# Expert weights with one run per partition, a moving operand read at a step of four, and another order of the state-space products

## The reference

```
h    = rmsnorm(x) ; proj = h @ w_in                      # 1024 x 5120
ya   = causal pooling mixer ; yb = gated MLP mixer
yc   = s5_mixer(...)                                     # 32 groups of 16 channels, 64 complex states
x    = x + (sum_k sigmoid(gate_k) * (y_k @ w_branch_k)) @ w_out
h2   = rmsnorm(x)
# 32 experts in 4 groups: best group, then 2 best experts in it, for each token
x    = x + sum over a token's 2 experts of weight * ((silu(h2 @ w_gate[e]) * (h2 @ w_up[e])) @ w_down[e])
out  = rmsnorm(x)
```

## Time and profile before

| | us |
|---|---|
| median of 3 runs | 930.88 |
| lowest and highest run | 930.44, 931.03 |
| the profiled execution | 932.56 |
| its span in the trace | 930.9 |
| PE busy in the span | 835.0 (90%) |
| DVE, ACT, POOL busy | 323.2, 195.7, 142.1 |
| bytes moved by DMA | 261.22 MB |

### The profile page before, as it was taken

The page is one execution under the profiler, slowest core; times in us unless marked ns, Lnnn a source line. Parts: engine busy times, 40 slices in busy tenths (PEclk is TensorE's granted clock), DMA queues, the critical chain, the costliest instruction groups (busy, mean ns, idle before and its releaser), DMA issues.

```text
span 930.9 us, 15236 instructions
## 1 busy us (share of the span) xinstructions
PE 835.0 (90%) x5300; PEld 569.9 (61%) x5301; DVE 323.2 (35%) x604; ACT 195.7 (21%) x289; POOL 142.1 (15%) x239
## 2 busy tenths in 40 slices
PE   7999999999999999989889998899999887777850
PEld 6888888868876888885555554555555444343420
DVE  4899996731524246265101111110101101010106
ACT  5633353222432233141000000000000000000002
POOL 4341601000000000012122221122112121212100
PEclk9999999999999999999999999999999999999995
DMA  8693224523224945049999999999999999999926
GB/s 263 148 186 111 75 66 44 167 69 113 91 90 153 401 148 225 1 160 387 402 417 420 418 418 420 421 420 419 418 420 419 419 420 421 420 420 420 410 118 268
DMA packets 77949, 261.22 MB, mean 281 GB/s; under 512 B 29260, under 2 KB 30284, under 8 KB 53300
## 3 DMA queue, kind: packets, MB, share of 16 engines
q1 hardware_dynamic: 71508, 249.91, 71.1%
q0 software_dynamic: 6256, 10.75, 3.1%
q10 hardware_dynamic: 144, 0.02, 0.0%
HBM read 254.76 MB, written 14.42 MB: 289 GB/s over the span
## 4 chain that ended last, share of the span: by engine, by line
PE 71%; SPq 15%; DVE 5%; DMA 4%; issue 2%; ACT 1%; POOL 0%; DVEq 0%; POOLq 0%; ACTq 0%
PE ps L1009 35%; PE ps L436 17%; SPq L421 14%; PE ps L449 9%; DMA au<-in_exp_w_up 4%; PE ps L994 3%; PE ps L986 1%; SPq L461 1%; PE ps L442 1%; DVE pair L655 1%; DVE pair L650 1%; DVE cv L700 1%; PE ps L1120 1%; PE ps L1148 1%; PE ps L1150 1%
## 5 line engine op out<-in xcount | busy, mean ns | idle before, releaser
L436 PE MATMUL ps<-ssm,pair 128*64 128x256 f32 x1120 | 127.2, 381 | 20.2 <-DMA ssm<-in_exp_w_gate 8.9
L650 DVE TENSOR_TENSOR pair<-pair,ps 128x256 f32<-128x256 f32 x32 | 13.5, 421 | 358.5 <-PE ps L436 358.5
L436 PEld LDWEIGHTS ps<-ssm,pair 128*64 128x64 f32 x1120 | 81.3, 137 | 71.1 <-issue 28.5
L1009 PE MATMUL ps<-h_hi,w_hi 128*128 128x512 f32 x280 | 109.6, 392 | 0.0
L1427 DVE TENSOR_TENSOR w_lo<-raw,w_hi 128x1024 fp32r<-128x1024 f32 x56 | 71.3, 1274 | 110.3 <-ACT w_hi L1236 109.5
L1009 PE MATMUL ps<-h_hi,w_lo 128*128 128x512 f32 x280 | 109.0, 389 | 0.0
L1009 PE MATMUL ps<-h_lo,w_hi 128*128 128x512 f32 x280 | 108.9, 389 | 0.0
L1236 ACT CAST w_hi<-raw 128x1024 fp32r<-128x1024 f32 x59 | 61.8, 1050 | 193.2 <-PE ps L1009 193.2
L714 ACT COPY late<-ps 128x512 f32<-128x512 f32 x35 | 20.5, 586 | 317.5 <-PE ps L449 317.5
L793 POOL DMA_INDIRECT choice_rows<-late,put_now x35 | 35.7, 1021 | 319.9 <-ACT late L714 284.1
L1009 PEld LDWEIGHTS ps<-h_hi,w_hi 128*128 128x128 f32 x280 | 52.6, 188 | 11.2 <-issue 0.4
(11 more groups left out here) (319 smaller groups left out, 1099.1 us busy)
## 6 DMA issues: line engine op xcount, KB each, us to landing
ssm<-in_exp_w_gate SPq DMA_DIRECT2D x22, 2048.0 KB, 29.4
au<-in_exp_w_up SPq DMA_DIRECT2D x11, 2048.0 KB, 30.0
ssm<-in_exp_w_up SPq DMA_DIRECT2D x11, 2048.0 KB, 33.7
ssm<-in_exp_w_down SPq DMA_DIRECT2D x11, 2048.0 KB, 33.9
hl<-in_exp_w_down SPq DMA_DIRECT2D x11, 2048.0 KB, 29.8
raw<-in_w_in SPq DMA_DIRECT2D x40, 512.0 KB, 3.8
hh<-in_exp_w_gate SPq DMA_DIRECT2D x10, 2048.0 KB, 28.4
mb<-in_exp_w_up SPq DMA_DIRECT2D x10, 2048.0 KB, 30.8
```

What stands on the lines that cost most here:

```text
L436: t = nc.tensor.matmul(ps[CAP * h:CAP * (h + 1), bank, 0:HALF], rows[:, k], w[:, k, HALF * h:HALF * (h + 1)], start=k == 0, stop=k == KD - 1)
L650: nc.vector.tensor_tensor(act_cols, silu_cols, up_now, ALU.mult).then_inc(act_ready, 1)
L1009: t = nc.tensor.matmul(bank, lhs, rhs, start=k == 0 and n == 0, stop=k == 2 * count - 1 and n == 2)
```

## The change

It does three things.

**Weights.** Partition p now has rows 8p to 8p+7 of gate and up and rows 4p to 4p+3 of down: one run of 16 KB per partition for each of the 2 MB loads, those of expert 0 too. So channel 8p + k of the tokens has to stand on partition p: `h2n` is written with its channels permuted (`halves`), the stored half row h holds channels 8q + 4h + j in the order (q, j), and `turn_x` stays as it is. Hidden channel 4c + 2h + j has to be column c of tile j of half h, so `hidden` reads its 256 columns as two lots of 128 at a step of four elements (16 bytes); in the kernel before its step was one. DVE's product of silu and up reads and writes in a row.

**Expert 0.** Its picked rows are made from `halves(x3)` (L542: four in a row, then a hop of eight), its four transposes read at a step of four, and they wait for both of ACT's copies where two of them waited for one. Its gain is `GFX` like that of all others.

**State-space output.** In a bank, the eight tap products come first and the sixteen state products behind them. The number of products is the same.

The core of the diff:

```diff
-        w_src = {"gate": exp_w_gate[0].rearrange("e (h p j) n -> e p h (j n)", p=P, j=4),
-                 "up": exp_w_up[0].rearrange("e (h p j) n -> e p h (j n)", p=P, j=4),
-                 "down": exp_w_down[0].rearrange("e (h p j) n -> e p h (j n)", p=P, j=2)}
+        w_src = {"gate": exp_w_gate[0].rearrange("e (p k) n -> e p (k n)", p=P),
+                 "up": exp_w_up[0].rearrange("e (p k) n -> e p (k n)", p=P),
+                 "down": exp_w_down[0].rearrange("e (p k) n -> e p (k n)", p=P)}
...
+        def halves(row):
+            return row.rearrange("p (q h j) -> p h q j", h=2, j=4)
...
         def hidden(rows, w_, kind, bank):
-            w = slot_k[EW[w_][kind]]
+            w = slot_k[EW[w_][kind]].rearrange("p k (c h j) -> p k h j c", h=2, j=2)
             for k in range(KD):
                 for h in range(2):
-                    t = nc.tensor.matmul(ps[CAP * h:CAP * (h + 1), bank, 0:HALF], rows[:, k],
-                                         w[:, k, HALF * h:HALF * (h + 1)], start=k == 0, stop=k == KD - 1)
+                    t = nc.tensor.matmul(ps[CAP * h:CAP * (h + 1), bank, 0:HALF].rearrange("p (j c) -> p j c", j=2), rows[:, k],
+                                         w[:, k, h], start=k == 0, stop=k == KD - 1)
...
-                    t = nc.tensor.matmul(ps[CAP * h:CAP * (h + 1), B_XT], place0[:, i], x3[:, i, W * h:W * (h + 1)],
+                    t = nc.tensor.matmul(ps[CAP * h:CAP * (h + 1), B_XT], place0[:, i], halves(x3[:, i])[:, h],
...
             for half in range(2):
                 pe.wait_ge(rows0_copied[half], 1)
-                for j in (2 * half, 2 * half + 1):
-                    t = nc.tensor.transpose(ps[:, B_AT, P * j:P * (j + 1)], rows0[:, P * j:P * (j + 1)], ident[:])
+            for j in range(4):
+                t = nc.tensor.transpose(ps[:, B_AT, P * j:P * (j + 1)], rows0.rearrange("r (p j) -> r j p", j=4)[:, j], ident[:])
...
-                nc.vector.tensor_tensor(act_cols, silu_cols, up_now, ALU.mult).then_inc(act_ready, 1)
+                nc.vector.tensor_tensor(act_, silu, up_now, ALU.mult).then_inc(act_ready, 1)
...
-                for q in range(4 * i, 4 * i + 4):
-                    outs = [bank[S * two:S * (two + 1), P * (q % 4):P * (q % 4 + 1)] for two in range(2)]
-                    halves = [slice(S * two, S * (two + 1)) for two in range(2)]
+                halves = [slice(S * two, S * (two + 1)) for two in range(2)]
+                outs = [[bank[rows, P * n:P * (n + 1)] for rows in halves] for n in range(4)]
+                for n in range(4):
                     for two in range(2):
-                        nc.tensor.matmul(outs[two], u8v[:, two * Q + q], toep[:, two * Q + q], start=True, stop=False)
-                    for two, rows in enumerate(halves):
-                        nc.tensor.matmul(outs[two], st_re[rows, q], cp_re[rows, q, 1:J + 1].rearrange("p j c -> p (j c)"), start=False, stop=False)
-                    for two, rows in enumerate(halves):
-                        t = nc.tensor.matmul(outs[two], st_im[rows, q], cp_im[rows, q, 1:J + 1].rearrange("p j c -> p (j c)"), start=False, stop=True)
+                        g = two * Q + 4 * i + n
+                        nc.tensor.matmul(outs[n][two], u8v[:, g], toep[:, g], start=n == 0, stop=False, skip_group_check=True)
+                for n in range(4):
+                    q = 4 * i + n
+                    for z, cp in ((st_re, cp_re), (st_im, cp_im)):
+                        for two, rows in enumerate(halves):
+                            t = nc.tensor.matmul(outs[n][two], z[rows, q], cp[rows, q, 1:J + 1].rearrange("p j c -> p (j c)"),
+                                                 start=False, stop=n == 3 and z is st_im, skip_group_check=True)
...
-                vv.tensor_scalar(h2n[i % 2], x3[:, i], stat[:, 50 + i:51 + i], None, ALU.mult).then_inc(h2_ready, 1)
+                vv.tensor_scalar(h2n[i % 2].rearrange("p (h q j) -> p h q j", h=2, j=4), halves(x3[:, i]), stat[:, 50 + i:51 + i], None,
+                                 ALU.mult).then_inc(h2_ready, 1)
```

More of the change, by code:

```diff
@@ L221, in trunk @@
         slot_h = [a.rearrange("p (k n) -> p k n", k=KF) for a in slots]
-        slot_runs = [a.rearrange("p (h n) -> p h n", h=2) for a in slots]
         NCP = Q * (J + 1) * CH
@@ L405, in trunk @@
         at_bank = ps[:, B_AT, 0:256].rearrange("p (j n) -> p j n", j=2)
-        up_now, silu_cols = (a.rearrange("p (c j) -> p j c", j=2) for a in (ps[:, B_UP, 0:F // 2], silu))
-        act_cols = act_.rearrange("p (j c) -> p j c", j=2)
+        up_now = ps[:, B_UP, 0:F // 2]
         rows0 = pair[:, 4096:4608]
@@ L410, in trunk, with turn_x @@
         HALF = F // 2
+        def halves(row):
+            return row.rearrange("p (q h j) -> p h q j", h=2, j=4)
         def weights(eng, w, kind, e, signal):
             src = w_src[kind][e] if isinstance(e, int) else w_src[kind][bass.ds(e, 1)]
-            dst = slot_runs[EW[w][kind]]
             if not isinstance(e, int):
[L417 to L423, removed]
+                src = src.rearrange("e p n -> (e p) n")
+            eng.dma_start(slots[EW[w][kind]], src).then_inc(signal, 16)
+        def turn_x(pe, rows, first=0, last=4):
             pe.sem_inc(passed, 1)
-            v = rows.rearrange(f"r {order} -> r j p", j=4)
+            v = rows.rearrange("r (p j) -> r j p", j=4)
             for j in range(first, last):
@@ L451, in down, with gain @@
             return t
-        def gain(rows, at=GFX):
+        def gain(rows, turned):
             return nc.vector.tensor_tensor(rows.rearrange("p (h j) t -> p j h t", h=2), turned,
-                                           cols[:, at:at + KD].rearrange("p (h j) -> p j h", h=2).unsqueeze(3).to_broadcast((P, 4, 2, CAP)),
+                                           cols[:, GFX:GFX + KD].rearrange("p (h j) -> p j h", h=2).unsqueeze(3).to_broadcast((P, 4, 2, CAP)),
                                            ALU.mult)
@@ L597, in turn, with second_block @@
                 second_block(e, w)
-            def second_block(e, w, order="(p j)"):
+            def second_block(e, w):
                 flag, before = second_of(pe, e)
@@ L604, in second_block @@
                     pe.wait_ge(xgT_ready, e + 2)
-                    turn_x(pe, xg2, order=order).then_inc(xt2_full, 1)
+                    turn_x(pe, xg2).then_inc(xt2_full, 1)
                     pe.wait_ge(xgT2_ready, before + 1)
@@ L613, in second_block @@
                     down(w, B_RES2).then_inc(done2["down"], 1)
-            second_block(0, 0, "(j p)")
+            second_block(0, 0)
             turn(1, 1, 0, 2, 1, True)
@@ L656, in turn @@
                 v.wait_ge(xt_full, e + 2)
-                gain(xgT).then_inc(xgT_ready, 1)
+                gain(xgT, turned).then_inc(xgT_ready, 1)
                 flag, before = second_of(v, e)
@@ L661, in turn @@
                     v.wait_ge(xt2_full, before + 2)
-                    gain(xgT2, GFF if first else GFX).then_inc(xgT2_ready, 1)
+                    gain(xgT2, turned).then_inc(xgT2_ready, 1)
                     v.wait_ge(silu2_ready, before + 1)
                     v.wait_ge(done2["up"], before + 2)
-                    nc.vector.tensor_tensor(act_cols, silu_cols, up_now, ALU.mult).then_inc(act2_ready, 1)
+                    nc.vector.tensor_tensor(act_, silu, up_now, ALU.mult).then_inc(act2_ready, 1)
                     v.wait_ge(at2_full, before + 1)
@@ L676, in over @@
                     v.wait_ge(done["up"], NE)
-                gain(xgT).then_inc(ov_xgT_ready, 1)
+                gain(xgT, turned).then_inc(ov_xgT_ready, 1)
                 v.wait_ge(ov_silu_ready, o_ + 1)
                 v.wait_ge(ov_done["up"], o_ + 1)
-                nc.vector.tensor_tensor(act_cols, silu_cols, up_now, ALU.mult).then_inc(ov_act_ready, 1)
+                nc.vector.tensor_tensor(act_, silu, up_now, ALU.mult).then_inc(ov_act_ready, 1)
                 v.wait_ge(ov_at_full, o_ + 1)
@@ L912, in _ @@
                 sp.dma_start(cols[:, at:at + k], v[0].rearrange("(k p) -> p k", p=P)).then_inc(consts_in, 16)
-            sp.dma_start(cols[:, GFX:GFX + KD].rearrange("p (h j) -> p h j", h=2),
-                         norm_ffn_g[0].rearrange("(h p j) -> p h j", h=2, j=4)).then_inc(consts_in, 16)
+            sp.dma_start(cols[:, GFX:GFX + KD], norm_ffn_g[0].rearrange("(p k) -> p k", p=P)).then_inc(consts_in, 16)
             full(sp, ("x", KD - 1))
@@ L1807, in _ @@
             v.wait_ge(xt_full, 1)
-            vv.tensor_tensor(xgT.rearrange("p (h j) t -> p j h t", h=2), turned0,
-                             cols[:, GFF:GFF + KD].rearrange("p (h j) -> p j h", h=2).unsqueeze(3).to_broadcast((P, 4, 2, CAP)),
-                             ALU.mult).then_inc(xgT_ready, 1)
+            gain(xgT, turned0).then_inc(xgT_ready, 1)
             for w in range(2):
```

## The result

The changed kernel takes 1151.61 us (four runs, 1150.53 to 1152.02) against 930.71 us (930.44 to 931.03): a ratio of 1.2367, 95% interval 1.2344 to 1.239. It is 221 us slower. The forecast was 923.5 us in a range to 960; the rival "strided reads double `hidden`" had 1136 us and a chance of 0.13.

A forecast was written before the change was run, and what follows sets the result against it. PE was taken to bound the kernel up to 399 us, then the stream of weight bytes. Sum: -4.1 (16 KB runs) - 3.4 (taps) + 0.1 (step) = -7.4 us, from 930.88 to 923.5 us; range 916 to 960 us.

The forecast's parts named there:

- strided reads double `hidden`: Rival: step-of-four reads take the gate and up products twice the time, 209 us more, 1136 us in all; chance 0.13.
- What bounds the kernel: TensorE bounds up to 399 us; the expert phase's end is set by the weight stream, from 413.23 to 891.8 us.
- The slack of PE: Expert phase: PE has 34 us to spare beside the weight stream, 1.05 us a block; past that PE is the bound.
- Part 1, 16 KB runs: Weight loads from expert 2 on: 16 KB packets in place of 8 KB save 4.1 us, at some 423 GB/s.
- The straight line: Packet cost fitted through the 2 KB and 8 KB rates: 0.0375 ns a byte and 5.7 ns a packet.
- Part 3, taps ahead of states: State-space output stage: fewer shape changes at 0.15 us each cut 15.25 us to 11.85, saving 3.4 us.
- The small edits: `h2n` writes, DVE's product, expert 0's transposes, the gather: `h2n` 0 to 1.3 us, gather 2.5 us later but hidden.
- Part 2, the step of four: Gate and up products' moving operand at 16-byte steps: at most 2% slower, mostly hidden, 0.1 us at the end.
- 0.2 us a block: Most that `hidden` was to lose per block: 2%, from 0.87 ns an element against 0.85 needed.
- the stated bound of 6.93: Worst case for `hidden` at the step of four: twice the time, 6.93 us more a block.
- a shared path: Possible mechanism for doubled `hidden`: the two side-by-side moving streams share one path, taking twice the time.
- a read for each pass: Possible mechanism for doubled `hidden`: the operand is read once for each of float32's passes, taking twice the time.

The follow-up runs named there:

- experiment 1: Kernel before with only the state-space output order changed (taps ahead of states): 928.18 us against 931.66, ratio 0.9962.
- experiment 4: Changed kernel, but each gate and up product reads its columns as 128 pairs of neighbours and DVE sorts the channels: 924.57 us, ratio 0.9922 to the kernel before.
- experiment 5: Kernel of experiment 4 with the old order of the state-space products (16 KB runs alone): 927.19 us against 932.26 for the kernel before, ratio 0.9943.
- experiment 3: Kernel before with the moving operand read at a step of two elements and DVE's product in a row: 930.94 us beside 931.66.
- experiment 6: Kernel before with gate and up products as one stream of 512 columns at a step of four, not two streams of 256 side by side: 1658.88 us.
- experiment 9: Two kernels with gate and up products on the words' upper halves as bf16: 454 ns a record pair at 16-byte step, 114 ns at 4 bytes; no whole time given.

## Why the prediction was wrong

*What bounds the kernel.* Right for the kernel before: in experiments 1, 4 and 5 the end moves with the start and the rate of the stream. The slack of PE was put at 34 us; PE's idle time fell by 35, and the subtraction above leaves some 39. That PE decides from 1.05 us a block on is borne out from both sides, though no run lies near it: 0.35 us more (experiments 3 and 4) cost nothing, and of 7.53 us more all but 1.1 us (39 us over 35 blocks) came off as loss.

*Part 1, 16 KB runs.* Right, but it could only be seen with the step taken out. Foretold 423 GB/s and 4.1 us; measured 423 and 424 GB/s, and 0.9943 of 930.7, 5.3 us (3.7 to 6.9 by the interval). The straight line through a 2 KB and an 8 KB rate carried to 16 KB.

*Part 3, taps ahead of states.* Right in mechanism and size: 11.85 us foretold for the stage, 11.67 measured; 3.4 us of time foretold, 3.5 measured.

*The small edits.* The forecast counts 0 us for the hops with which `h2n` is written. No row of before showed that; in the changed kernel's trace `h2n` is written in 0.753 us for 0.75. DVE's product takes 0.42 us as before. But expert 2's load was foretold for 409.8 us and went out at 411.10: for 0.77 us of that DVE waited for an earlier store of half rows before it could write the last `h2n`, a wait of which the other float32 kernels' traces have 0.3 us at most (experiment 4: none, and 410.36 us). A gather lands in 8.6 us (median, experiment 4) for 6.8, 1.8 us later where 2.5 were foretold; one of them, for an early block, keeps PE waiting for 0.9 us, and in the changed kernel none does.

*Part 2, the step of four, is the step that failed.* The sentence is "the pace is the same as in the nearest rows": the pace of a stationary load at 16 bytes, 0.87 ns an element from the earlier trace rows, was carried over to the moving operand and compared with the 0.85 ns that it needs. The moving operand's own pace at that step is 1.77 ns. Half of the rate was missing: the term "0.2 us a block" measured 7.53, which is beyond even the stated bound of 6.93, and there are 35 blocks of it. The two ways named in which it could take twice the time (a shared path, a read for each pass) failed as mechanisms, experiments 6 and 9, so it was in part luck that the size which the rival drew from them was near: 1136 us for 1152. The products grew by a factor of 2.09 and not 2, 21 us more, and some 5 us more of them were hidden.

What the step costs in float32 is told by the elements that the stream finds in a line: two of them cost 5% (7.28 against 6.93 us for the 64 records), one costs 109% (14.46 us).

The range failed for the same cause. It gave an unmeasured resource a likeliest value with two digits and left the bound of +6.93 us a block outside, although nothing in the trace excluded it; two other parts that could be read well made the sum look surer than its weakest term.

What stays open: why the stationary load reads a strided line about twice as fast as the moving operand (both figures are from traces, no run took them apart), what a single bf16 stream costs at this step, and the 2% between steps of four and eight.

## What to carry to other kernels

Count the 16-byte lines of a moving operand, not its step: keep at least two float32 elements of each line in a stream (7.28 us for the 64 records here, 14.46 with one), and put the rest of a permutation where it is free, here in DVE's 0.42 us product, which costs the same at a step of two as in a row (421 ns in both). The rate of the stationary load told nothing of the moving operand (0.87 against 1.77 ns a line): where the whole sum hangs on one unmeasured rate, give the bad bound its full weight. When a change with three parts loses much, time its parts apart before giving it up: two of them were worth 0.8% together, and the kernel of experiment 4 keeps both.

## What the runs showed of the hardware

In each record a moving operand that found one element in a 16-byte line took 1.77 ns a line (1.80 at a step of eight). That was the same for float32 and bf16 with two streams side by side (452 and 454 ns for a pair of records), for one float32 stream alone (1.76 ns) and for two, with a DMA share of 0.97 or of 0.02 (float32, 14.46 us a block in both), and at a granted clock of 1.00 or 0.50 (bf16, 7.44 us a block in both). With two elements in a line a float32 product took 0.89 ns a column, within 5% of the 0.85 ns that it takes with no step; bf16 at 0.45 ns a column had four. Packets of 16 KB raised a full stream of loads from 419 to 423 and 424 GB/s (experiments 5 and 4). On the array, going between 128-row and 64-row products cost 0.15 us each time, so 32 changes brought down to 8 were worth 3.6 us of the stage (15.25 to 11.67), and 3.5 us of the whole time (experiment 1).
